# Wider modulation blocks and an earlier return of solved blocks in a two-layer hybrid attention and delta-rule trunk

## Chip, core and metric

One core of one Trainium2 chip runs the whole program. The metric is the device time in microseconds; the median of three runs of the kernel before is 2593.26.

## Reference

Two layers over 512 tokens (256 context, 256 latent) of width 2048, all in float32. Each layer computes a modulation (shift, scale and gate, 3 x 2048 columns each for latent and context) from two conditioning vectors, one input projection, two groups of eight heads (differential attention with rotary positions; a gated delta rule in both directions with a short convolution), and one output projection:

```
mod_lat = silu(c) @ w_ada + b_ada;  mod_ctx = silu(c_ctx) @ w_ada + b_ada
p  = (rmsnorm(x, norm_w) * (1 + sc) + sh) @ w_in
y_a = diff_post(diff_attend(q_l, k_all, v_all, lam), subln_w, lam_init, za)
m = tril_strict((k_beta @ k.T) * decay) + eye      # 64-token chunks
sol = triangular_solve(m, [v * beta, k_beta * exp(g)])
x  = x + gt * (concat([y_a, y_b]) @ w_out)
```

The context is updated in layer 0 only; layer 1 computes outputs for the latent tokens alone. The result is the RMS-normed latent stream.

## The kernel before

Engines are programmed one by one, and semaphores order them. A head of the input projection has eight tiles of 128 columns (AV, BQ, BK, AQ, AK, ZA, BV, ZB), each of two units of 8 x 128 rows: 16 units, 64 slots of four to a unit. In each slot TensorE does two row blocks of three matmuls (L1699 to L1701: w_hi by h_hi, w_hi by h_lo, w_lo by h_hi), and then what a hand-written plan puts into that slot for the head before ("fill"): transposes, Gram matrices (L1769, L1771), the merge of the inverse (L1780, L1789, L1790), the state recurrence, scores (L1858), the turn of the attention weights (L1865) and their product (L1872). ScalarE, VectorE, GpSimd and SyncE run the same slots with lists of their own, each in strict order of its list. A layer is nine bodies: projection of head 0 without fill, seven with both, and the last with the output projection in place of the input one.

Weights: SyncE loads a unit into one of two raw buffers (L526, `w_raw`) as soon as the unit two before it has been split; ScalarE rounds it to w_hi (L607, `split_hi`), VectorE subtracts for w_lo (L1060, `split_lo`), both three units ahead of TensorE (`LEAD`).

The inverse of the delta rule starts from 16 x 16 blocks. SyncE takes them to partitions through DRAM (L540, L543, `blocks_to_partitions`, in front of the load of unit 7), VectorE solves them in slots 12 to 15 of layer 0 (L293 to L309), SyncE brings them back (L548, L553, `blocks_back`, in front of the load of unit 10), and VectorE transposes them (L1312) in slots 20 and 21. TensorE's first merge step (L1780) is at slot 22.

Modulation columns that are not needed at the start (layer 0's gate, layer 1's all) are made in 64 blocks of 128 columns, six a head in layer 0 (slots 9, 14, 18, 46, 51, 57) and two a head in layer 1 (10, 17). For each block ScalarE loads 2048 x 128 weights in two DMAs (L912), TensorE multiplies with 16 matmuls of 32 columns on four column strips (L1639), ScalarE copies the result (L626) and issues the next load, TensorE turns it (L1648), and VectorE adds the bias. The first three blocks of a head in layer 0 use PSUM banks G0 and G1, the others A0 and A1.

In the last body the output projection's tiles n go to PSUM bank PJ + n % 2 (L1959 to L1961). ScalarE loads x (`part_load`, L933), VectorE adds gate x product (L1517), ScalarE stores (`part_store`, L944). The two head rows that come last are multiplied after it, in 16 products (L1998 to L2000), each followed by VectorE's add (L1517), ScalarE's square (L1033) and GpSimd's running sum (L1602), which the next RMS norm needs (L1661). A table of decay factors is made at the start of each layer in slots 2 to 8 of its first body (`table_step`, L1724, L1732, L1737). In layer 1 the first two units are multiplied before that body, so its first eight slots hold no projection.

Of the kernel before, what the change touches and what calls it, by code (L numbers as in the profile page):

```python
# [150 lines left out]
def build_trunk(nc, x, c, ctx_in, c_ctx, w_ada, b_ada, norm_w, w_in, conv_w, dn_a_log, dn_dt_bias,  # L151
# [15 lines left out]
    with ExitStack() as ctx:  # L167
# [28 lines left out]

        arena_size = 20764
        arena = sb("arena", [P, arena_size])
# [112 lines left out]
        def ada_banks(early):  # L311
            return (bank(G0, P), bank(G1, 2)) if early else (bank(A0, P), bank(A1, 2))

# [126 lines left out]
        def last_unit(n):  # L440

            return n + 2 if n < 2 else 2 * n + 1

        def piece_slot(p):
# [154 lines left out]
        def _(act):  # L599
# [23 lines left out]
            def ada_copy(value, early):  # L623
                act.wait_ge(ada_used, value * 2)
                need(act, ada_turned, value - 1)
                nc.scalar.copy(ada_sb[:], ada_banks(early)[0]).then_inc(ada_copied, 1)  # L626
                act.wait_ge(ada_copied, value)
# [48 lines left out]
            for layer in range(DEPTH):  # L676
# [56 lines left out]
                def body(i, project, fill):  # L733
# [170 lines left out]
                    def ada(k):  # L904
                        ada_copy(i * ADA_IN[layer] + (ada_before(layer) + k + 1), k < ADA_EARLY[layer])
                        if k + 1 < ADA_IN[layer]:
                            ada_load(k + 1)

                    def ada_load(k):
                        lay, firstb = ada_block(layer, k)  # L910
                        for hf in range(2):
                            act.dma_start(ada_raw[:, hf], w_ada[lay].rearrange("(k p) n -> p k n", p=P)[  # L912
                                :, hf * HALF:(hf + 1) * HALF, bass.ds((i * 2 + (firstb + k % 2)) * P, P)]).then_inc(
                                    ada_loaded[RAW + hf], 16)
# [63 lines left out]
                    if project:  # L978
                        for t in (AV, BQ, BK, AK, BV):
                            put(8 * t + 8, evacuate, t)  # L980
                        put(8 * AQ + 8, evacuate, AQ)
                        put(22, tanh, 0)
                        put(30, tanh, 1)
                        put(62, tanh, 2)
                        put(8 * ZA + 8, evacuate_z, 0, ZA)
                        put(0, ada_load, 0)
                        for k, s in enumerate(ADA_SLOT[layer]):
                            put(s + 1, ada, k)
                        if isinstance(i, int) and i == 0:
                            put(3, table_step, 0)  # L990
                            put(6, table_step, 1)
                            put(8, table_step, 2)
                            put(12, load_g, 0, 0)
                    if not project:
                        put(63, y_hi_last, 1)
                        for n in range(KT):
                            put(out_slot(n), part_store, n)
                            if n + 4 < KT:
                                put(min(out_slot(n) + 2, SLOTS - 1), part_load, n + 4)
                        for u in range(OUT_UNITS):  # L1000
                            put(piece_slot(2 * u), split_hi, 0, first + u + LEAD, OUT_HEADS if u + LEAD < OUT_UNITS else HALF)
                    for s in range(SLOTS):
                        if project and s % 4 == 1:
                            split_hi(i, base + 2 + s // 4 + LEAD)
                        for f, a in plan.get(s, ()):
                            f(*a)
# [48 lines left out]
        def _(vec):  # L1055
# [28 lines left out]
            def mod_column(value, lay, blk, early):  # L1084

                vec.wait_ge(ada_turned, value)
                tt(mod[:, lay, bass.ds(blk, 1), :].rearrange("p o v -> p (o v)"), ada_banks(early)[1],
                   vecs[:, 1, bass.ds(blk + lay * 3 * KT, 1)].to_broadcast([P, 2]), ALU.add).then_inc(mod_ready, 1)
                vec.wait_ge(mod_ready, value)
# [67 lines left out]
            for layer in range(DEPTH):  # L1157
# [49 lines left out]
                def body(i, project, fill):  # L1207
# [215 lines left out]
                    def ada(k):  # L1423
                        lay, firstb = ada_block(layer, k)
                        mod_column(i * ADA_IN[layer] + (ada_before(layer) + k + 1), lay, i * 2 + (firstb + k % 2),
                                   k < ADA_EARLY[layer])
# [56 lines left out]
                    if project:  # L1483
# [7 lines left out]
                        for k, s in enumerate(ADA_SLOT[layer]):  # L1491
                            put(s + 3, ada, k)
                        if isinstance(i, int) and i == 0:
                            put(2, table_step, 0)
                            put(4, table_step, 1)
                            put(6, table_step, 2)
                            put(8, table_step, 3)
                    if not project:
# [14 lines left out]
                def add_product(n, dst):  # L1513

                    for v in range(c0 // 2, 2):
                        seg = slice(v * N_CTX, (v + 1) * N_CTX)
                        m = V.scalar_tensor_tensor(dst[:, seg], ps[:, PJ + n % 2, seg], mod[:, layer, 2 * KT + n, v:v + 1],  # L1517
                                                   dst[:, seg], ALU.mult, ALU.add)
# [92 lines left out]
        def _(pe):  # L1611
# [18 lines left out]

            def ada_multiply(slots, loads, prior, out_):

                need(pe, ada_copied, prior)
                for half in range(2):
                    pe.wait_ge(slots[half][1], loads[half])
                    for k in range(HALF):
                        kt = half * HALF + k
                        j = kt % 4
                        last = mm(out_[32 * j:32 * j + 32], c_T[:, kt, :], slots[half][0][:, k, :],  # L1639
                                  start=kt < 4, stop=kt >= KT - 4)  # L1640
                        if k == HALF - 1:
                            last.then_inc(ada_used, 1)

            def ada_turn(value, out_):

                pe.wait_ge(ada_copied, value)
                need(pe, mod_ready, value - 1)
                mm(out_, ada_sb[:], sel, start=True, stop=True).then_inc(ada_turned, 1)  # L1648

# [37 lines left out]
            for layer in range(DEPTH):  # L1687
# [52 lines left out]
                def body(i, project, fill):  # L1740
# [150 lines left out]
                    def ada(k):  # L1891
# [6 lines left out]
                        loads = [i * (16 * ADA_IN[layer]) + 16 * (at_start[hf] + n + 1) for hf in range(2)]  # L1898
                        sl = [(ada_raw[:, hf], ada_loaded[RAW + hf]) for hf in range(2)]
                        v = i * ADA_IN[layer] + (first_loads + k)  # L1900
                        ada_multiply(sl, loads, v, ada_banks(k < ADA_EARLY[layer])[0])

# [31 lines left out]
                    if project:  # L1934
                        for n, s in enumerate(ROTATE[layer]):
                            put(s, rotate, n)
                        for k, s in enumerate(ADA_SLOT[layer]):
                            put(s, ada, k)
                            put(s + 2, ada_t, k)
                        if isinstance(i, int) and i == 0:  # L1940
                            put(2, table_step, 0)
                            put(5, table_step, 1)
                            put(8, table_step, 2)
                    def out_piece(p):
# [3 lines left out]
                        if p % 2 == 0:  # L1948
                            pe.wait_ge(w_split, u + 1)
                        if p == 0:  # L1950
                            pe.wait_ge(evacuated, (layer + 1) * LAYER_TILES)
                        if p % 2 == 0 and half == 0 and n >= 2:
                            pe.wait_ge(out_added, layer * 2 * KT + n - 1)
                        for k in (range(0, 4), range(4, OUT_HEADS))[p % 2]:
                            kt = half * HALF + k
                            if n == 0:
                                pe.wait_ge(y_split, layer * Y_STEPS + y_group_of[kt] + 1)
                            o = ps[:, PJ + n % 2, c0 * P:]
                            mm(o, w_hi[:, u % SPLIT, k], h_hi[:, kt, c0 * P:], start=kt == 0, stop=False)  # L1959
# [29 lines left out]
                for n in range(KT):  # L1989
# [4 lines left out]
                    for m, k in enumerate((OUT_HEADS, OUT_HEADS + HEADS)):  # L1994
                        hi, lo = [w[:, u % SPLIT].rearrange("p k n -> p (k n)")[:, (4 * m + col) * P:(4 * m + col + 1) * P]
                                  for w in (w_hi, w_lo)]
                        o = ps[:, PJ + n % 2, c0 * P:]
                        mm(o, hi, h_hi[:, k, c0 * P:], start=m == 0, stop=False)  # L1998
# [42 lines left out]
```

## Time and profile before

| | |
|---|---|
| median of the runs | 2593.26 us (2592.95 to 2595.0) |
| the profiled execution | 2584.58 us |
| its span | 2582.8 us |
| mean granted clock of TensorE | 0.963 |
| TensorE matmul busy | 2337.6 us, 91% |
| a filled head of layer 0, from one L1780 wait to the next (594.68 to 742.11) | 147 us |
| VectorE, ScalarE, GpSimd busy | 54%, 36%, 5% |
| DMA, mean | 128 GB/s |

The span runs from the first to the last instruction of the profiled execution. Times in rows are microseconds from its start, and durations in microseconds unless they are called ns. Busy shares are means over stages that differ.

### The profile page before, as it was taken

How to read it: one execution, taken by the hardware profiler on the slowest of the kernel's cores; microseconds unless marked ns; L12 is line 12 of the kernel's file. 1: busy time of each engine (PE TensorE's matmuls, PEld its weight loads, DVE VectorE, ACT ScalarE, POOL GpSimd, SP SyncE). 2: the span in 40 equal slices, each digit the busy share in tenths (PEclk: the TensorE clock that was granted, in tenths of full speed). 3: DMA queues.
4: the chain of work that ended last, by engine and by line, in shares of the span. 5: the costliest groups of instructions: out<-in, count | busy, mean ns of one | idle time of the engine just before them, and what ended most of it. 6: DMA issues, size and time to landing. Idle time of an engine off the chain costs nothing. (4 is left out here: it accounts for less than half of the span.)

```text
span 2582.8 us, 40809 instructions
## 1 busy us (share of the span) xinstructions
PE 2337.6 (91%) x14870; PEld 1931.1 (75%) x14870; DVE 1394.7 (54%) x2377; ACT 927.3 (36%) x1727; POOL 136.8 (5%) x187
## 2 busy tenths in 40 slices
PE   6799898998989898998999878999999999999687
PEld 3278786877768686877778757788887878878686
DVE  1343655555454555555564354656566665766554
ACT  3433324242423324242422253433424244242423
POOL 0000000000001000000100020000000000000002
PEclk8899999999999999999999989999999999999898
DMA  8964434352434445252545415533434344343453
GB/s 321 353 188 130 111 107 126 89 134 78 123 100 124 110 110 131 73 149 73 168 121 160 147 57 156 127 102 96 128 83 120 91 108 113 96 122 92 129 154 105
DMA packets 553603, 329.72 MB, mean 128 GB/s; under 512 B 48658, under 2 KB 517814, under 8 KB 552710
## 3 DMA queue, kind: packets, MB, share of 16 engines
q1 hardware_dynamic: 393174, 218.59, 30.5%
q10 hardware_dynamic: 160240, 109.13, 14.4%
q8 instruction: 94, 1.54, 0.2%
q14 instruction: 31, 0.25, 0.0%
q0 software_dynamic: 64, 0.20, 0.0%
HBM read 304.73 MB, written 23.13 MB: 127 GB/s over the span
## 5 line engine op out<-in xcount | busy, mean ns | idle before, releaser
L1699 PE MATMUL ps<-h_hi,w_hi 128*128 128x512 f32 (+1 forms) x2080 | 825.9, 397 | 17.6 <-DVE w_lo L1060 7.6
L1700 PE MATMUL ps<-h_lo,w_hi 128*128 128x512 f32 (+1 forms) x2080 | 765.1, 368 | 0.0
L1701 PE MATMUL ps<-h_hi,w_lo 128*128 128x512 f32 (+1 forms) x2080 | 764.2, 367 | 0.0
L1060 DVE TENSOR_TENSOR w_lo<-w_raw,w_hi 128x1024 fp32r<-128x1024 f32 (+1 forms) x332 | 399.2, 1202 | 345.9 <-ACT w_hi L607 280.0
L607 ACT CAST w_hi<-w_raw 128x1024 fp32r<-128x1024 f32 (+1 forms) x332 | 341.8, 1030 | 441.0 <-PE ps L1701 142.4
L1699 PEld LDWEIGHTS ps<-h_hi,w_hi 128*128 128x128 f32 x2080 | 398.4, 192 | 110.0 <-issue 42.6
L1701 PEld LDWEIGHTS ps<-h_hi,w_lo 128*128 128x128 f32 x2080 | 396.3, 191 | 67.5
L1700 PEld LDWEIGHTS ps<-h_lo,w_hi 128*128 128x128 f32 x2080 | 398.8, 192 | 46.5
L1060 DVE TENSOR_TENSOR arena<-arena,ps 128x512 f32<-128x512 f32 (+1 forms) x192 | 117.6, 640 | 107.4 <-PE ps L1790 106.0
L1959 PE MATMUL ps<-h_hi,w_hi 128*128 128x512 f32 (+1 forms) x448 | 160.6, 359 | 15.5 <-ACT arena L773 10.6
L1780 PE MATMUL ps<-arena 128*128 128x128 f32 x768 | 110.4, 290 | 55.6 <-DVE arena L1312 55.6
L1961 PE MATMUL ps<-h_hi,w_lo 128*128 128x512 f32 (+1 forms) x448 | 154.5, 345 | 0.0
L1960 PE MATMUL ps<-h_lo,w_hi 128*128 128x512 f32 (+1 forms) x448 | 154.4, 345 | 0.0
L1780 PEld LDWEIGHTS ps<-arena 128*128 128x128 f32 x768 | 104.7, 203 | 65.3 <-DVE arena L1312 60.6
L1559 POOL TENSOR_SCALAR small<-small 128x4 f32<-128x4 f32 (+3 forms) x51 | 20.5, 402 | 2358.9 <-DVE small L1413 1060.2
L1228 DVE SCALAR_TENSOR_TENSOR arena<-arena,convh 128x512 f32<-128x512 f32 (+1 forms) x192 | 135.7, 707 | 7.0 <-DVE arena L309 1.0
L1790 PE MATMUL ps<-arena 128*128 128x128 f32 x768 | 132.7, 275 | 0.0
L848 ACT ACTIVATE arena<-ps,hcol 128x128 f32<-128x128 f32 x128 | 40.1, 364 | 208.5 <-PE ps L1808 208.5
L1790 PEld LDWEIGHTS ps<-arena 128*128 128x128 f32 x768 | 111.1, 192 | 2.5
L1959 PEld LDWEIGHTS ps<-h_hi,w_hi 128*128 128x128 f32 x448 | 88.6, 198 | 27.7 <-issue 14.7
L1789 PE MATMUL ps<-arena 128*128 128x128 f32 x512 | 99.6, 276 | 6.5 <-DVE arena L1060 6.5
L1961 PEld LDWEIGHTS ps<-h_hi,w_lo 128*128 128x128 f32 x448 | 88.5, 198 | 9.2
(191 smaller groups left out, 2740.4 us busy)
## 6 DMA issues: line engine op xcount, KB each, us to landing
w_raw<-in_w_in SPq DMA_DIRECT2D x260, 512.0 KB, 4.1
ada_raw<-in_w_ada ACTq DMA_DIRECT2D x128, 512.0 KB, 5.1
w_raw<-in_w_out SPq DMA_DIRECT2D x64, 448.0 KB, 3.7
arena<-in_w_ada SPq DMA_DIRECT2D x27, 512.0 KB, 8.3
w_raw<-in_w_ada SPq DMA_DIRECT2D x19, 512.0 KB, 8.5
ada_raw<-in_w_ada SPq DMA_DIRECT2D x18, 512.0 KB, 8.3
arena<-decay_rows ACTq DMA_DIRECT2D x16, 512.0 KB, 5.7
x_channel_major<-arena ACTq DMA_DIRECT2D x1, 4096.0 KB, 17.5
```

The source lines that it names most:

```text
L607: nc.scalar.copy(w_hi[:, u % SPLIT, 0:tiles], w_raw[:, s, 0:tiles]).then_inc(w_hi_ready, 1)
L1060: return V.tensor_tensor(o, a, b, op)
L1228: m = V.scalar_tensor_tensor(acc, src, w, acc, ALU.mult, ALU.add)
L1699: mm(o, w_hi[:, s, k], h_hi[:, kt, t0:], start=kt == 0, stop=False)
L1700: before_last = mm(o, w_hi[:, s, k], h_lo[:, kt, t0:], start=False, stop=False)
L1701: last = mm(o, w_lo[:, s, k], h_hi[:, kt, t0:], start=False, stop=kt == KT - 1)
L1780: last = mm(quads(GX[d])[:, cc], m_T[:, d, cc], inv[:, d, cc], start=True, stop=True)
L1789: mm(quads(GX[d])[:, cc], inv_T[:, d, cc], prod[:, d, cc], start=True, stop=True)
L1790: last = mm(quads(GT[d])[:, cc], prod[:, d, cc], inv_T[:, d, cc], start=True, stop=True)
L1959: mm(o, w_hi[:, u % SPLIT, k], h_hi[:, kt, c0 * P:], start=kt == 0, stop=False)
L1960: mm(o, w_hi[:, u % SPLIT, k], h_lo[:, kt, c0 * P:], start=False, stop=False)
L1961: last = mm(o, w_lo[:, u % SPLIT, k], h_hi[:, kt, c0 * P:], start=False, stop=kt == HALF + OUT_HEADS - 1)
```

## The change

- Modulation: 32 pairs of blocks in place of 64 blocks. Each slot now holds one half of the contraction for 256 columns (8 matmuls, two DMAs with rows twice as long); copy, turn (two matmuls) and add come once a pair. Slots in layer 0 are 9, 12, 16, 19, 46, 52 with the first four in the early banks, in layer 1 10 and 16.
- `blocks_back` stands in front of the load of unit 9 in layer 0, not of unit 10.
- Output projection: tile n uses bank PJ + (n + 1) % 2; tile 0 waits for all but the last of the projection's tiles to be copied, tile 1 for the last. ScalarE's list has its splits in front of stores; stores come one slot after the add and loads three slots later than before.
- Layer ends: VectorE's split stands behind the add of n = 2, 6, 10, 14, not in front of the add of n = 0, 4, 8, 12.
- The table of layer 1 is made in slots 9 to 15.

```diff
-        ada_sb = sb("ada_sb", [P, P])
+        ada_sb = sb("ada_sb", [P, 2 * P])
...
-        arena_size = 20764
+        arena_size = 20488
...
-        ADA_SLOT, ADA_EARLY = {0: (9, 14, 18, 46, 51, 57), 1: (10, 17)}, {0: 3, 1: 2}
-        BLOCKS_OUT, BLOCKS_BACK = {0: 7, 1: 7}, {0: 10, 1: 10}
+        TABLE = {0: 0, 1: 7}
+        ADA_SLOT, ADA_EARLY = {0: (9, 12, 16, 19, 46, 52), 1: (10, 16)}, {0: 4, 1: 2}
+        BLOCKS_OUT, BLOCKS_BACK = {0: 7, 1: 7}, {0: 9, 1: 10}
...
+        def out_bank(n):
+            return PJ + (n + 1) % 2
...
                     def ada(k):
-                        ada_copy(i * ADA_IN[layer] + (ada_before(layer) + k + 1), k < ADA_EARLY[layer])
+                        value = i * ADA_IN[layer] + (ada_before(layer) + k + 1)
+                        act.wait_ge(ada_used, value * 2)
+                        if k % 2:
+                            ada_copy(value, k < ADA_EARLY[layer])
                         if k + 1 < ADA_IN[layer]:
                             ada_load(k + 1)
...
-                        for n in range(KT):
-                            put(out_slot(n), part_store, n)
-                            if n + 4 < KT:
-                                put(min(out_slot(n) + 2, SLOTS - 1), part_load, n + 4)
                         for u in range(OUT_UNITS):
                             put(piece_slot(2 * u), split_hi, ...)
+                        for n in range(KT):
+                            put(min(out_slot(n) + 1, SLOTS - 1), part_store, n)
+                        for n in range(KT - 4):
+                            put(min(out_slot(n) + 5, SLOTS - 1), part_load, n + 4)
...
                 for n in range(KT):
                     if n % 4 == 0:
-                        if n == 0 or layer < DEPTH - 1:
-                            split_lo(0, first + OUT_UNITS + n // 4 + LEAD)
                         vec.wait_ge(old_loaded[n // 4], 16 * (layer + 1))
                     vec.wait_ge(last_product, layer * KT + n + 1)
                     add_product(n, xT[:, n])
                     vec.wait_ge(out_added, (2 * layer + 1) * KT + n + 1)
+                    if n % 4 == 2 and (n == 2 or layer < DEPTH - 1):
+                        split_lo(0, first + OUT_UNITS + n // 4 + LEAD)
...
-            def ada_multiply(slots, loads, prior, out_):
+            def ada_multiply(half, loads, prior, out_):
                 need(pe, ada_copied, prior)
-                for half in range(2):
-                    pe.wait_ge(slots[half][1], loads[half])
-                    for k in range(HALF):
-                        kt = half * HALF + k
+                for hf in range(2):
+                    pe.wait_ge(ada_loaded[RAW + hf], loads[hf])
+                    for j in range(HALF // 2):
+                        kt = half * HALF + hf * HALF // 2 + j
...
-                        if p == 0:
+                        if p % 2 == 0 and half == 0 and n == 0:
+                            pe.wait_ge(evacuated, (layer + 1) * LAYER_TILES - 1)
+                        if p % 2 == 0 and half == 0 and n == 1:
                             pe.wait_ge(evacuated, (layer + 1) * LAYER_TILES)
```

## Rows read from the trace of the kernel before

**Rows 1.** The page, busy time, share and instructions of each engine.
```profile
PE 2337.6 (91%) x14870; PEld 1931.1 (75%) x14870; DVE 1394.7 (54%) x2377; ACT 927.3 (36%) x1727; POOL 136.8 (5%) x187
```
**Rows 2.** Waits of TensorE, whole span: total us, times, longest.
```profile
PE ps L1959 <- ACT arena L773: 10.6, 2, 5.5
PE ps L1639 <- DMA ada_raw<-in_w_ada: 7.9, 9, 1.7
...
PE ps L1732 <- DVE arena L1190: 7.5, 2, 7.0
```
**Rows 3.** Waits of TensorE, 290 to 1195, the filled heads of layer 0.
```profile
PE ps L1780 <- DVE arena L1312: 52.0, 7, 7.9
PE ps L1865 <- DVE arena L1407: 8.4, 6, 2.9
```
**Rows 4.** Timeline, 576 to 600: start, duration, instruction, [idle before it].
```profile
578.43 0.19 DVE L309 TENSOR_SCALAR arena<-arena 64x64 f32<-64x64 f32 x1
...
580.51 1.02 ACTq L912 DMA_DIRECT2D ada_raw<-in_w_ada  x2
...
581.82 0.37 SPq L526 DMA_DIRECT2D w_raw<-in_w_in  x1
582.24 0.90 SPq L548 DMA_DIRECT2D s_blocks<-arena  x1
...
588.91 3.64 SPq L553 DMA_DIRECT2D arena<-s_blocks  x8
593.91 0.71 DVE L1312 STREAM_TRANSPOSE arena<-arena 128x512 f32<-128x512 f32 x1 [9.86 <-DMA arena<-s_blocks]
...
594.68 2.07 PE L1780 MATMUL ps<-arena 128*128 128x128 f32 x8 [7.92 <-DVE arena L1312]
```
**Rows 5.** DMA issues: count, KB each, median us to landing.
```profile
w_raw<-in_w_in SPq DMA_DIRECT2D x260, 512.0 KB, 4.1
ada_raw<-in_w_ada ACTq DMA_DIRECT2D x128, 512.0 KB, 5.1
...
s_blocks<-arena SPq DMA_DIRECT2D x16, 64.0 KB, 1.9
```
**Rows 6.** Timeline, 556 to 575: a modulation load and who waits.
```profile
561.65 1.02 ACTq L912 DMA_DIRECT2D ada_raw<-in_w_ada  x2
...
562.28 0.48 SPq L543 DMA_DIRECT2D arena<-m_blocks  x1
...
567.43 0.64 PE L1639 MATMUL ps<-ada_raw,c_T 128*32 128x128 f32 x16
568.62 0.17 DVE L293 TENSOR_TENSOR arena<-arena 64x14 f32<-64x14 f32 x1 [4.18 <-DMA arena<-m_blocks]
...
568.91 0.65 PE L1639 MATMUL ps<-ada_raw,c_T 128*32 128x128 f32 x16 [0.83 <-DMA ada_raw<-in_w_ada]
```
**Rows 7.** Windows: busy PE, PEld, DVE, ACT, POOL; granted clock; DMA share, GB/s.
```profile
594.00:599.00 5.00, 4.32 (x17) 3.85 (x18) 4.33 (x8) 0.63 (x1) 0.00 (x0) 0.57 0.00 0
```
**Rows 8.** Timeline of TensorE, 653 to 656: a turn.
```profile
654.36 0.37 PE L1648 MATMUL ps<-cst,ada_sb 128*128 128x2 f32 x2
654.59 0.48 PE L1699 MATMUL ps<-h_hi,w_hi 128*128 128x512 f32 x1
```
**Rows 9.** Timeline, 1466 to 1512, the end of layer 0.
```profile
1473.68 0.79 PE L1998 MATMUL ps<-h_hi,w_hi 128*128 128x512 f32 x1 [4.81 <-DVE arena L1517]
...
1482.50 1.23 DVE L1060 TENSOR_TENSOR w_lo<-w_raw,w_hi 128x1024 fp32r<-128x1024 f32 x1 [2.37 <-ACT w_hi L607]
...
1510.73 1.44 PE L1661 MATMUL ps<-cst,arena 128*128 128x1 f32 x6 [3.47 <-POOL arena L1602]
```
**Rows 10.** Groups by line and form, GpSimd: busy us, mean ns, idle before.
```profile
L1602 POOL TENSOR_TENSOR arena<-arena 128x512 f32<-128x512 f32 x16 | 20.5, 1281 | 41.3 <-ACT arena L1033 40.7 <-POOL arena L1602 0.2
```
**Rows 11.** Timeline, 2436 to 2448, output part of layer 1.
```profile
2439.79 1.09 DVE L1060 TENSOR_TENSOR w_lo<-w_raw,w_hi 128x896 fp32r<-128x896 f32 x1 [2.09 <-ACT w_hi L607]
...
2447.03 1.12 PE L1865 MATMUL ps<-cst,arena 128*128 128x128 f32 x4 [7.51 <-DVE arena L1407]
```

More of the change, by code:

```diff
@@ L1491, in body @@
                         for k, s in enumerate(ADA_SLOT[layer]):
-                            put(s + 3, ada, k)
+                            if k % 2:
+                                put(s + 3, ada, k)
                         if isinstance(i, int) and i == 0:
[L1494 to L1497, printed above, removed]
+                            put(TABLE[layer] + 2, table_step, 0)
+                            put(TABLE[layer] + 4, table_step, 1)
+                            put(TABLE[layer] + 6, table_step, 2)
+                            put(TABLE[layer] + 8, table_step, 3)
                     if not project:
@@ L1629, in turn_x @@
                     last.then_inc(x_turned, 1)
-            def ada_multiply(slots, loads, prior, out_):
+            def ada_multiply(half, loads, prior, out_):
                 need(pe, ada_copied, prior)
-                for half in range(2):
-                    pe.wait_ge(slots[half][1], loads[half])
-                    for k in range(HALF):
-                        kt = half * HALF + k
-                        j = kt % 4
-                        last = mm(out_[32 * j:32 * j + 32], c_T[:, kt, :], slots[half][0][:, k, :],
+                for hf in range(2):
+                    pe.wait_ge(ada_loaded[RAW + hf], loads[hf])
+                    for j in range(HALF // 2):
+                        kt = half * HALF + hf * HALF // 2 + j
+                        last = mm(out_[32 * j:32 * j + 32], c_T[:, kt, :], ada_wide_rows(hf)[:, j],
                                   start=kt < 4, stop=kt >= KT - 4)
-                        if k == HALF - 1:
-                            last.then_inc(ada_used, 1)
+                    last.then_inc(ada_used, 1)
             def ada_turn(value, out_):
                 pe.wait_ge(ada_copied, value)
-                need(pe, mod_ready, value - 1)
-                mm(out_, ada_sb[:], sel, start=True, stop=True).then_inc(ada_turned, 1)
+                need(pe, mod_ready, value - 2)
+                for b in range(2):
+                    last = mm(out_[:, 2 * b:2 * b + 2], ada_sb[:, b * P:(b + 1) * P], sel, start=True, stop=True)
+                last.then_inc(ada_turned, 2)
             pe.wait_ge(staged, 2)
@@ L1898, in ada @@
                         loads = [i * (16 * ADA_IN[layer]) + 16 * (at_start[hf] + n + 1) for hf in range(2)]
-                        sl = [(ada_raw[:, hf], ada_loaded[RAW + hf]) for hf in range(2)]
-                        v = i * ADA_IN[layer] + (first_loads + k)
-                        ada_multiply(sl, loads, v, ada_banks(k < ADA_EARLY[layer])[0])
+                        v = i * ADA_IN[layer] + (first_loads + k // 2 * 2)
+                        ada_multiply(k % 2, loads, v, ada_banks(k < ADA_EARLY[layer])[0])
                     def ada_t(k):
@@ L1938, in body @@
                             put(s, ada, k)
[L1939 removed]
+                            if k % 2:
+                                put(s + 2, ada_t, k)
                         if isinstance(i, int) and i == 0:
[L1941 to L1943 removed]
+                            put(TABLE[layer] + 2, table_step, 0)
+                            put(TABLE[layer] + 5, table_step, 1)
+                            put(TABLE[layer] + 8, table_step, 2)
                     def out_piece(p):
```

34 lines of the change are left out of this document (18 added, 16 removed).

## Prediction

> **What bounds the kernel now.** I read the page first: the reader is to see that TensorE is busy 91% of the span, with VectorE at 54% and ScalarE at 36% [rows 1]. No other engine is near its limit, so the time is TensorE's work plus the stretches in which it stands still, and an edit counts only if it shortens one of these. The second view is therefore the waits of TensorE over the whole span [rows 2] and over the heads of layer 0 [rows 3]. Of its idle time after start-up, the largest single item is 52.0 us: seven waits, one in each filled head of layer 0, for the transpose of the solved blocks (L1312). Each is 7 to 8 us in a head of 147 us. All the others named in [rows 2, 3] are 4 to 15 us in total. The third view is the timeline of one such head, to see what the wait hangs on; the fourth the granted clock behind it; the rest are the same for each other edit.
>
> **1. Blocks back one unit sooner.** In [rows 4] VectorE ends the substitution at 578.6. SyncE's queue has the load of unit 9 in front of the solved blocks (unit count of the head), and that load waits for a split until 581.82; the store of the blocks goes out at 582.24, is waited for until 588.91, the eight reads take 3.64 to issue, and the transpose runs at 593.91, 1.36 after the last issue. TensorE then goes on at 594.68, after 7.92 idle. With the blocks in front of load 9 the store goes out at about 578.7. A store with nothing in its way lands in 1.9 [rows 5], so: 578.7 + 1.9 + 3.7 + 1.4 = 585.7, plus 0.7 for the transpose = 586.4. TensorE reached the place at 594.68 - 7.92 = 586.76. So the wait could go wholly. It is not free of company: in the store's way at 582.24 were the weight load of 581.82 and a modulation load of ScalarE's queue at 580.51, and it took 6.7 instead of 1.9. In the new order the load of the fourth modulation piece is issued by ScalarE at about 577 to 578 (slot 17), just ahead of the store. I leave 5 of the 52 (0.7 a head) and take **-47**; bounds: -52 (all gone), and -25 if the store still takes 6.7 at 578.7, which would leave about half. What is moved back is weight load 9: it now stands behind the store, its wait and eight reads, so it goes out near 585 instead of 581.8. It is split at slot 25, three slots (2.3 us each, 147 by 64) after the place at which TensorE waited, so at about 593.5; with 4.1 to land [rows 5] there are some 4 to 5 us to spare, and I cost it at nothing. GpSimd's queue is not touched.
> On what lies in a transfer's way the Trainium skill says otherwise than these rows ("DMA: Bandwidth & Descriptors", section "Queues, rings and completion order"): each DMA engine takes turns between the queues that have work, packet by packet, so ScalarE's loads would slow the small store but not hold it. By that the five left over go as well and the blocks come in sooner too; this is rival B. The rows do not bear it out well: the read of the blocks issued at 562.28, behind two ScalarE loads at 561.65, was used only at 568.62 [rows 6].
>
> **2. The clock behind those waits.** Between 594 and 599 the granted clock is 0.57 [rows 7]: TensorE had been idle for 7.9, and then ran near its 1.2 GHz level for most of them; the mean of the span is 0.963. With 4.32 busy in these 5 us, 4.32 x 0.43 = 1.86 is lost; I take 1.75, seven times: **-12** (bounds 0 and -14). It comes only if the wait becomes short; how long an idle time leaves the clock alone these rows do not show, so the near bound is 0.
>
> **3. Modulation pieces of 256 columns.** The 64 blocks become 32 pairs; each pair is two calls (half of the contraction each), one copy, one turn of two matmuls, one add. A call had 32 instructions on 128 columns and now has 16 on 256: the same columns, 0.65 for each half call [rows 6]. Turns: one turn takes 0.23 until the next matmul starts [rows 8]; a pair took 0.46, now one start and twice the instructions, about 0.35: 32 x 0.11 = 3.5. I take **-4** with a little for fewer instructions (bounds 0 and -8). Copies and adds lie on engines with room.
> The DMAs carry the same bytes. But slots change in layer 0 from 9, 14, 18, 46, 51, 57 to 9, 12, 16, 19, 46, 52. A load is issued by ScalarE one slot after a piece and must be in at the next: it had 4 slots from 9 to 14 and now has 2 from 9 to 12, and 2 from 16 to 19. In [rows 6] the load issued at 561.65 is what TensorE waits for at 568.91 (idle 0.83), 7.3 later; that piece was at slot 14 and began at 567.43; two slots of 6 x 0.23 and a turn sooner, slot 12 comes at 567.43 - 2.8 - 0.3 = 564.3. The median of these loads is 5.1, that of a weight load 4.1 [rows 5]; I take 4.7 for the landing, between the two, as it now ends before the weight load behind it begins. Issued 0.4 sooner, as no copy is in front, it is in at 566.0, and the second half (wanted at 564.8) waits 1.2. The waits for this load were 7.9 in all [rows 2]; I put 1.2 at slot 12 and 0.2 to 0.5 at slot 19 in seven heads, and 3 to 4 in the unfilled first one: about 15, so **+7** (bounds -5, if longer rows land sooner, and +25, if it lands 7.3 after issue as in [rows 6]). In layer 1 the second piece moves from slot 17 to 16 with over 2 us in hand: nothing. The add of the first block left the substitution's way and the blocks arrive sooner, so the wait for VectorE's mix at L1865 (8.4 [rows 3]) should halve, and with it some clock: **-5** (bounds 0 and -8).
>
> **4. Layer ends.** In layer 0's last 16 products VectorE splits w_lo ahead of every fourth add. At 1482.50 it starts this 2.37 late, waiting for ScalarE's half, which itself comes only after the last square; the add comes behind it, and TensorE waits for the add. The first wait of this kind is 4.81, at 1473.68 [rows 9]. The split now comes two adds later, when w_hi has long been there. What is late next: GpSimd's running sum, 16 x 1.28 [rows 10] = 21 with its gaps, and TensorE's 6 x 0.23 = 1.4 a product. The sum ended for TensorE at 1510.73. Started at 1472 and paced at 1.4 to 1.5, it ends at 1495 to 1496: -15. Layer 1 has only the first of these splits and half the tokens; of the 4.81 I take -3 for it. Together **-18** (bounds -10 and -21).
>
> **5. Output part.** Tile 0 now goes to the other PSUM bank and no longer waits for z_b's copy: 10.6 in two waits [rows 2]. What ends last then is the split of y (h_lo), made by the same two engines just before the copy; no row parts the two, so the bounds are 0 and -10.6, and as the code hands both out in slots 0 and 1 I take a small part: **-3**. ScalarE's split no longer queues behind a store that waits for the add. In layer 0's output part TensorE has no wait for it: nothing. In layer 1's it idles 7.51 [rows 11] for VectorE's mix, and 7 us before its end VectorE had itself stood 2.09 for such a split; two or three of them go by half, with the smaller waits around: **-5** (0 to -9). The stores go out one slot later and the loads three later; a part loaded 5 slots after tile n is used some 15 slots after it, so this is covered.
>
> **6. Table of layer 1** moves 7 slots. There the first 8 slots have no projection, so TensorE idled 7.05 for L1190 (7.5 with layer 0's [rows 2]). It can now start unit 2 when VectorE has split it, about 2.4 after the last unit; slots 9 to 15 have 256 columns only and give back 1 to 2: **-4** (0 to -7).
>
> **Sum:** -47 - 12 - 4 + 7 - 5 - 18 - 3 - 5 - 4 = -91. The profiled execution took 2584.6 (span 2582.8 and 1.8 around it), so 2493.6 in its terms. The median of the runs is 8.7 above it, 2593.3: forecast **2502**. All best bounds together give -52 - 14 - 8 - 5 - 8 - 21 - 10.6 - 9 - 7 = -135, 2459; the terms do not err together, and half of that distance either way, 2480 to 2524, is the likely one's own range.
>
> **Rivals.**
> A, forecast. 0.55.
> B, the two queues share and nothing holds the blocks: L1780 and L1865 waits go wholly, -5 and -3.4 more: about 2493. For it: no row shows a small transfer in front of a load being slow. Against: [rows 6]. 0.16.
> C, the blocks are still late: store behind the fourth piece's load, the reads beside the fifth's. Each head keeps 3 to 4 us idle and the clock dip: -25 and 0 in place of -47 and -12: 2502 + 34 = about 2536. For it: 6.7 for a 64 KB store in [rows 4]. 0.14.
> D, the modulation loads become the wait of layer 0: 4.9, their whole landing, exposed at slots 12 and 19, less what the blocks' wait hid: 7 x (9.8 - 1.7) = +57 on my +7 term, minus 7 x 0.7: about 2554. For it: only two slots each. Against: slots there carry fillers and last over 2 us. 0.08.
> E, within 0.2%: the idle time is only handed from one wait to the next in each head. 0.03.
> F, slower: SyncE stands in front of weight load 9 until the blocks are solved. If the substitution ended more than 5 us later than now, load 9 would starve the split, and as two raw buffers chain the loads, every unit behind it. To eat 91 in seven heads it must end 18 us later (5 to spare and 91 / 7 = 13 of loss); nothing in [rows 4, 6] is that late. At 20 it gives about 2607. 0.04.
> Measurement can tell about 0.2% (5 us) from no change. Faster 0.93, same 0.03, slower 0.04. The range 2478 to 2540 takes in A, B and C, about 85%.
>
> **What would show it.** Right: L1780's wait for L1312 in layer 0 under 1 us a head; granted clock 1.00 where it was 0.57; the store of s_blocks some 3 us before the weight load; L1639's wait for its DMA grown to about 15; the last GpSimd sum of layer 0 within 25 us of the first; L1732 near nothing. Wrong: the store landing more than 5 us after issue (C); L1639 waits above 4 us (D); a wait of L1699 for w_lo near slot 36 (F); or a new wait in slots 22 to 33, where VectorE and TensorE hand the merge back and forth in every slot and which the old wait gave VectorE time for.

## The result, and the profile after

The changed kernel took 2517.3 us (median; 2515.01 to 2523.75), the kernel before 2593.1 beside it: ratio 0.9716, interval 0.9697 to 0.9735, 76 us or 2.8% faster. The forecast was 2502 with 2478 to 2540. The direction and the range held, and the gain is some 15 short of the 91 of the sum. The profiled execution took 2515.0 against 2584.6, 69.6 less. That the range held is in part luck: terms of the sum that came out too large and others that came out too small offset each other; which ones is what the experiments ask.

The page, busy time of each engine (answers to [rows 1]):
```profile
PE 2322.5 (92%) x13846; PEld 1893.7 (75%) x13846; DVE 1392.0 (55%) x2345; ACT 922.2 (37%) x1695; POOL 147.3 (6%) x187
```
TensorE has 15 us less of work, the instructions saved by wider blocks and some time at the full clock; the rest of the gain is idle time. Waits of TensorE over the whole span (answers to [rows 2, 3]; L1651 is the old L1639, L1793 the old L1780, L1878 the old L1865, L1974 the old L1959, L1745 the old L1732, L1712 the old L1699):
```profile
PE ps L1878 <- DVE arena L1419: 29.3, 16, 7.1
PE ps L1793 <- DVE arena L1324: 17.4, 9, 3.5
...
PE ps L1974 <- DVE h_lo L1072: 13.1, 6, 4.2
PE ps L1651 <- DMA ada_raw<-in_w_ada: 12.8, 17, 1.5
...
PE ps L1674 <- POOL arena L1615: 8.9, 2, 6.3
...
PE ps L1745 <- DVE arena L1202: 5.4, 1, 5.4
PE ps L1660 <- ACT ada_sb L634: 5.3, 7, 1.0
```
and in the window 290 to 1147, the filled heads of layer 0:
```profile
PE ps L1793 <- DVE arena L1324: 15.0, 7, 3.5
PE ps L1651 <- DMA ada_raw<-in_w_ada: 9.2, 12, 1.2
PE ps L1802 <- DVE mod L1072: 3.2, 3, 1.2
```
The 52.0 us of the blocks became 15.0, not 5. The L1865 waits of these heads (8.4 in [rows 3]) are gone. L1651 waits grew by 5, as forecast. Two waits are new: L1802 for the pair's add on VectorE, and L1660 for ScalarE's copy of the pair in layer 1.

One head of layer 0 in the timeline shows why 15 are left (answers to [rows 4]; L557 and L562 are the blocks' store and reads, L535 the weight load, L924 the modulation load):
```profile
561.87 0.94 ACTq L924 DMA_DIRECT2D ada_raw<-in_w_ada  x2
562.45 0.19 DVE L309 TENSOR_SCALAR arena<-arena 64x64 f32<-64x64 f32 x1
562.72 0.47 SPq L557 DMA_DIRECT2D s_blocks<-arena  x1
...
566.96 3.65 SPq L562 DMA_DIRECT2D arena<-s_blocks  x8
...
569.93 0.94 ACTq L924 DMA_DIRECT2D ada_raw<-in_w_ada  x2
...
570.93 8.06 SPq L535 DMA_DIRECT2D w_raw<-in_w_in  x2
...
573.91 0.71 DVE L1324 STREAM_TRANSPOSE arena<-arena 128x512 f32<-128x512 f32 x1 [5.83 <-DMA arena<-s_blocks]
...
574.67 1.16 PE L1793 MATMUL ps<-arena 128*128 128x128 f32 x8 [1.75 <-DVE arena L1324]
```
The store now goes out 0.1 behind the solve, as forecast. But a modulation load of 1 MB (two DMAs of 512 KB, the weights of one modulation slot or "piece") was issued 0.9 ahead of it, and the store is done 4.2 after its issue, not 1.9; the next modulation load goes out among the last reads, and the transpose comes 3.3 behind the last issue, not 1.4. From the solved blocks to the transpose it is 11.3 us where the forecast had 7.1 and the kernel before 15.3.

The granted clock behind three of these waits (answers to [rows 7], with its columns; the clock is the third number from the end):
```profile
436.10:441.10 5.00, 5.00 (x23) 4.56 (x24) 4.54 (x8) 0.63 (x1) 0.00 (x0) 0.66 0.36 101
574.70:579.70 5.00, 4.77 (x28) 3.93 (x28) 4.54 (x8) 0.63 (x1) 0.00 (x0) 1.00 0.34 94
713.50:718.50 5.00, 4.80 (x28) 3.93 (x28) 4.54 (x8) 0.63 (x1) 0.00 (x0) 1.00 0.39 111
```
Idle times of 1.85, 1.75 and 1.79 precede them. The first was followed by most of 5 us at the 1.2 GHz level, the other two were not. In four of the seven heads the clock was at 0.66 to 0.69, in three at 1.00.

### The profile page after: what moved, and what is told of

The parts are those of the page before. It is cut to its first block and busy times, and to the rows that moved or that the text cites. A ratio compares the mean times of both kernels' runs of the same rounds, so it can differ in the third digit from the quotient of the medians.

```text
span 2513.2 us, 38542 instructions
## 1 busy us (share of the span) xinstructions
PE 2322.5 (92%) x13846; PEld 1893.7 (75%) x13846; DVE 1392.0 (55%) x2345; ACT 922.2 (37%) x1695; POOL 147.3 (6%) x187
## 5 line engine op out<-in xcount | busy, mean ns | idle before, releaser
L1712 PE MATMUL ps<-h_hi,w_hi 128*128 128x512 f32 (+1 forms) x2080 | 824.3, 396 | 19.1 <-DVE w_lo L1072 10.9
L1712 PEld LDWEIGHTS ps<-h_hi,w_hi 128*128 128x128 f32 x2080 | 399.1, 192 | 123.0 <-issue 52.4
L1713 PEld LDWEIGHTS ps<-h_lo,w_hi 128*128 128x128 f32 x2080 | 399.9, 192 | 47.7
L1974 PE MATMUL ps<-h_hi,w_hi 128*128 128x512 f32 (+1 forms) x448 | 160.0, 357 | 13.4 <-DVE h_lo L1072 13.1
L1803 PE MATMUL ps<-arena 128*128 128x128 f32 x768 | 132.6, 275 | 0.0
L1793 PE MATMUL ps<-arena 128*128 128x128 f32 x768 | 105.2, 281 | 17.4 <-DVE arena L1324 17.4
L1793 PEld LDWEIGHTS ps<-arena 128*128 128x128 f32 x768 | 100.6, 196 | 25.5 <-DVE arena L1324 20.8
L1802 PE MATMUL ps<-arena 128*128 128x128 f32 x512 | 99.7, 276 | 10.6 <-DVE arena L1072 7.4
L1974 PEld LDWEIGHTS ps<-h_hi,w_hi 128*128 128x128 f32 x448 | 87.8, 196 | 26.7 <-issue 12.5
```

What stands on the lines that cost most here:

```text
L1712: mm(o, w_hi[:, s, k], h_hi[:, kt, t0:], start=kt == 0, stop=False)
L1713: before_last = mm(o, w_hi[:, s, k], h_lo[:, kt, t0:], start=False, stop=False)
L1793: last = mm(quads(GX[d])[:, cc], m_T[:, d, cc], inv[:, d, cc], start=True, stop=True)
L1802: mm(quads(GX[d])[:, cc], inv_T[:, d, cc], prod[:, d, cc], start=True, stop=True)
L1803: last = mm(quads(GT[d])[:, cc], prod[:, d, cc], inv_T[:, d, cc], start=True, stop=True)
```

## The experiments

Twelve runs. The kernel before was measured in each group: 2589.1, 2588.8 and 2591.4. Times across groups are compared by ratio. The changed kernel, run again unedited in the second group, had 0.9704; with the first 0.9716 I take 0.971, and a ratio higher by 0.001 is 2.6 us. By the intervals, a difference from the changed kernel is known to about 0.002, 5 us, either way.

| run | median us | ratio | interval |
|---|---|---|---|
| blocks_alone | 2546.9 | 0.9834 | 0.9816 to 0.9851 |
| table_unmoved | 2521.5 | 0.9736 | 0.9721 to 0.9751 |
| piece_17 | 2512.3 | 0.9707 | 0.9685 to 0.9728 |
| pieces_15_18 | 2525.8 | 0.9750 | 0.9735 to 0.9766 |
| after_again | 2512.3 | 0.9704 | 0.9689 to 0.9718 |
| small_loads | 2472.2 | 0.9540 | 0.9521 to 0.9559 |
| table_15 | 2512.4 | 0.9713 | 0.9692 to 0.9735 |
| pieces_15_19 | 2501.2 | 0.9657 | 0.9642 to 0.9672 |
| ends_unmoved | 2537.4 | 0.9788 | 0.9775 to 0.9802 |
| out_undone | 2525.1 | 0.9750 | 0.9735 to 0.9765 |
| mended | 2503.5 | 0.9659 | 0.9646 to 0.9672 |
| blocks_undone | 2536.9 | 0.9791 | 0.9776 to 0.9806 |

**The blocks, done alone and undone.** Two runs.
```diff
 # blocks_alone: the kernel before
-BLOCKS_OUT, BLOCKS_BACK = {0: 7, 1: 7}, {0: 10, 1: 10}
+BLOCKS_OUT, BLOCKS_BACK = {0: 7, 1: 7}, {0: 9, 1: 10}
 # blocks_undone: the changed kernel
-BLOCKS_OUT, BLOCKS_BACK = {0: 7, 1: 7}, {0: 9, 1: 10}
+BLOCKS_OUT, BLOCKS_BACK = {0: 7, 1: 7}, {0: 10, 1: 10}
```


> The kernel before with one edit: solved blocks come back in front of load 9 in layer 0. Theory (what is left of the wait in the changed kernel comes from ScalarE's modulation loads, which now go out 0.9 us ahead of the store and just ahead of the last read): with the old slots the load nearest to the store is issued 1.8 us behind it, so the store lands in about 2 us, L1780 waits under 1.2 us in each head of layer 0, and the granted clock behind it is near 1.00: about 2539 (-54). Rival (the solved blocks need 12 us from the last step of the solve to TensorE whatever stands beside them): L1780 waits 1.8 to 3.5 in each head, the clock still falls in half of them: about 2549 (-44).

> The changed kernel with the blocks back in front of load 10, as before. Theory (the edit is worth 42 us alone, and the other edits of layer 0 do not depend on it): L1793 waits 6 to 8 a head, about 2554 (+42). Rival (with the new slots the modulation load goes out before load 9 and the blocks, so the late blocks cost more): over 2560. Rival of the other side (TensorE comes to the place later by the pieces' waits, which hide part): under 2545.

Alone the edit gave 42 to 43 us, so the rival's number held. Its reason held only in part: the old slots leave the store free (first read 2.0 behind the solve), but the modulation load that follows it at 1.8 goes out just ahead of the reads. In this run's timeline the transpose comes 9.8 behind the end of the solve at 566.73:
```profile
566.54 0.19 DVE L309 TENSOR_SCALAR arena<-arena 64x64 f32<-64x64 f32 x1
566.81 0.47 SPq L548 DMA_DIRECT2D s_blocks<-arena  x1
...
568.62 1.05 ACTq L912 DMA_DIRECT2D ada_raw<-in_w_ada  x2
568.75 4.76 SPq L553 DMA_DIRECT2D arena<-s_blocks  x8
...
576.53 0.71 DVE L1312 STREAM_TRANSPOSE arena<-arena 128x512 f32<-128x512 f32 x1 [4.37 <-DMA arena<-s_blocks]
...
577.30 1.16 PE L1780 MATMUL ps<-arena 128*128 128x128 f32 x8 [2.42 <-DVE arena L1312]
```
Taken back out of the changed kernel it cost only 21 (0.9791 less 0.971), half as much, and the rival of the other side had the right number. The waits of TensorE in blocks_undone, 290 to 1180:
```profile
PE ps L1793 <- DVE arena L1324: 32.2, 7, 5.1
PE ps L1651 <- DMA ada_raw<-in_w_ada: 10.4, 13, 2.4
```
So the new slots of the pieces had already taken the blocks' wait from 52.0 to 32.2, with the blocks where they were. Two things show in its timeline. TensorE comes to the place some 10 to 11 behind the solve instead of 8. And the modulation load that had stood 1.7 ahead of the late store [rows 4] now goes out 3.3 ahead of it (4.4 to 5.5 in five other heads), and the store and its wait take 4.2 (3.8 to 4.0 there) instead of 6.7. What it still waits behind is the weight load of its own queue, issued 0.4 ahead of it. Times from issue to landing (us, last number) of the three transfers, first in the kernel before (issued 580.4 to 583), then in blocks_undone (573.3 to 577.5):
```profile
ada_raw<-in_w_ada ACTq DMA_DIRECT2D x2, 512.0 KB, 6.1
w_raw<-in_w_in SPq DMA_DIRECT2D x1, 512.0 KB, 6.9
s_blocks<-arena SPq DMA_DIRECT2D x1, 64.0 KB, 6.7
```
```profile
ada_raw<-in_w_ada ACTq DMA_DIRECT2D x2, 512.0 KB, 4.2
w_raw<-in_w_in SPq DMA_DIRECT2D x1, 512.0 KB, 4.4
s_blocks<-arena SPq DMA_DIRECT2D x1, 64.0 KB, 4.1
```
In both the store lands 0.1 to 0.2 behind that weight load (588.9 against 588.7, 580.9 against 580.8), and well behind the modulation load. The two edits take from the same wait, and the sum counted it once for each.

**Where the modulation loads stand.** Three runs on the changed kernel:
```diff
 # pieces_15_18, and pieces_15_19
-ADA_SLOT = {0: (9, 12, 16, 19, 46, 52), 1: (10, 16)}
+ADA_SLOT = {0: (9, 12, 15, 18, 46, 52), 1: (10, 16)}
+ADA_SLOT = {0: (9, 12, 15, 19, 46, 52), 1: (10, 16)}
 # small_loads, in ada_load
+few = 1 if layer == 0 else HALF // 2
-act.dma_start(ada_wide_rows(hf), w_ada...[:, first_k:first_k + HALF // 2, ...])
+act.dma_start(ada_wide_rows(hf)[:, :few], w_ada...[:, first_k:first_k + few, ...])
```


> The changed kernel with the third and fourth modulation pieces of layer 0 at slots 15 and 18, not 16 and 19. Theory (the store of the blocks is held by the load that is issued 0.9 us ahead of it): that load now goes out some 3 us ahead, the store lands in about 2 us, L1793 waits 0 to 0.5 in place of 1.8 a head and the clock no longer falls behind it: about 2502 (-15). Rival: the load of the fifth piece then stands in front of the eight reads, the idle time stays: within 3 of 2517.

> The changed kernel, but every modulation load in the heads of layer 0 brings only one of its four row blocks, a quarter of the bytes; TensorE multiplies what lies in the buffer, so the modulation is not that of the reference. Theory (the modulation loads hold the blocks' store and reads, and are themselves what L1651 waits for): L1651 waits under 2 in place of 12.8, L1793 under 2 in place of 17.4, and the clock does not fall behind it: about 2487 (-30). Rival (the blocks' way through DRAM is slow by itself, and the loads only make the pieces wait): L1793 keeps 15 and more, about 2506 (-11).

> The changed kernel with the third modulation piece of layer 0 at slot 15, not 16; its load then goes out some 3 us ahead of the blocks' store, not 0.9, and the fourth piece keeps slot 19. Theory (a load of 1 MB takes 4 to 5 us, and what stands behind it waits for the rest): the first read comes some 3 us after the solve in place of 4.4, L1793 waits under 0.5 a head, L1651 grows by 0.4 to 0.8 a head at slot 15: about 2507 (-10). Rival (idle time is only handed to L1651, as with slots 15 and 18, where its waits grew by 27): 2517 or more.

With slots 15 and 18 the blocks' wait for VectorE went away as expected and the kernel still became 10 us slower. The waits of TensorE from 290 to 1170 in pieces_15_18, and from 290 to 1147 in pieces_15_19:
```profile
PE ps L1651 <- DMA ada_raw<-in_w_ada: 32.9, 33, 2.7
```
```profile
PE ps L1651 <- DMA ada_raw<-in_w_ada: 19.0, 25, 2.2
```
Neither has a row for L1793 left. In the first, both the third and the fourth piece have two slots from issue to use, and the idle time of the blocks is handed to the pieces with more on top: the prediction's rival D, at a smaller size. In the second, three slots lie before slot 19: L1651 grows from 9.2 to 19.0, but L1793 loses its 15.0, and the time fell by 14 (0.9657; 11 in medians of the same group). The expectation had the right number with a wrong picture of the order: the load goes out 0.8 behind the store, not 3 ahead of it:
```profile
566.16 0.18 DVE L309 TENSOR_SCALAR arena<-arena 64x64 f32<-64x64 f32 x1
566.43 0.47 SPq L557 DMA_DIRECT2D s_blocks<-arena  x1
...
567.23 0.95 ACTq L924 DMA_DIRECT2D ada_raw<-in_w_ada  x2
568.36 3.65 SPq L562 DMA_DIRECT2D arena<-s_blocks  x8
...
573.89 0.71 DVE L1324 STREAM_TRANSPOSE arena<-arena 128x512 f32<-128x512 f32 x1 [0.84 <-DMA arena<-s_blocks]
...
577.80 1.05 PE L1793 MATMUL ps<-arena 128*128 128x128 f32 x8
```
Here the chain is what the forecast had: read 2.0 behind the end of the solve (566.34), transpose 7.6, against a forecast of 7.1, and TensorE does not wait. The granted clock is 1.00 in the five us behind L1793 in all seven heads. With a quarter of the bytes (small_loads, which leaves out three quarters of these weights, so that its result is not the reference's) no wait at all is left in this stretch, neither for the blocks nor for the pieces. One head, from 411.7:
```profile
411.70:544.50 132.80, 132.80 (x792) 107.58 (x791) 78.72 (x132) 48.16 (x96) 6.55 (x9) 1.00 0.31 86
```
TensorE is busy for all 132.8 us, at full clock, where a head of the changed kernel takes 138.0 to 139.4. The transpose comes 7.2 to 7.7 behind the solve, in place of 11.3. The 44 us of small_loads below the changed kernel (40 in medians of the group, where its expectation had 30) are the whole price of these loads, waits, clock and unfilled head together. That settles the cause: the way of the blocks through DRAM is not slow by itself.

**Layer 1's second piece, and the table.** Three runs on the changed kernel:
```diff
 # piece_17
-ADA_SLOT = {..., 1: (10, 16)}
+ADA_SLOT = {..., 1: (10, 17)}
 # table_unmoved, and table_15
-TABLE = {0: 0, 1: 7}
+TABLE = {0: 0, 1: 0}
+TABLE = {0: 0, 1: 15}
```


> The changed kernel with the second modulation piece of a head of layer 1 at slot 17, as before, not 16. Theory: ScalarE's copy of the pair stands in slot 17 behind the exponentials of the second scores and TensorE's turn in slot 18 waits for it 0.9 us a head; one slot later nothing is in front of it: L1660 waits near 0 and 5 to 8 us less, about 2511. Rival: the loss of layer 1 (8.3 us over its heads) comes from elsewhere, a copy of 256 columns and a turn of two matmuls; then 2517.

> The changed kernel with the table of layer 1 in slots 2 to 8, as before. The prediction's step: the move gave 4 us, so this is 4 slower, 2521. Rival, from the two traces set side by side at the same projection matmul (65.8 us ahead in front of the table, 64.4 behind it): the move gave nothing or cost 1.4, as the chain through ScalarE's two loads of a function table is as long as three short slots in either place: 2516 to 2517.

> The changed kernel with the table of layer 1 in slots 17 to 23, not 9 to 15; these slots have 512 columns. Theory (the chain of the table through VectorE and ScalarE takes some 9 us and is covered only by slots that long): L1745 waits under 1 in place of 5.4, 5 to 8 us less, about 2510. Rival (ScalarE's and VectorE's part of the chain delays the splits and copies of the head instead): within 2 of the changed kernel.

piece_17 took the wait L1660 away, and its median did not move (0.9707 against 0.971); in its trace six heads of layer 1 take 654.4 together, in the changed kernel's second execution 655.8, a difference too small for the medians. The loss of layer 1 that it was to mend was partly no property of the kernel: set side by side at the same projection matmul, the first execution of the changed kernel lost 8.3 us on the kernel before over the heads of layer 1, the second only 2.7. The difference comes in steps of 1.5, one head each. The same 110.9 us of both (changed kernel, then again):
```profile
1856.50:1967.40 110.90, 104.25 (x678) 89.07 (x677) 69.64 (x121) 41.73 (x81) 6.92 (x9) 0.98 0.37 104
```
```profile
1856.50:1967.40 110.90, 104.04 (x688) 89.89 (x687) 70.88 (x123) 41.73 (x81) 6.93 (x9) 1.00 0.38 104
```
Beside the first head, where every trace has 0.98, the clock fell in three heads of the first and in none of the second. What stays is 0.4 us a head, some 3 in all, which the forecast had at nothing.

table_unmoved was 7 slower (0.9736), 5 either way, so the sign of the forecast's step (4) held and its size is not contradicted, but its reason did not hold. TensorE waits 5.35 for the table's chain in the new place and 6.94 in the old one, but by slot 15 the old place is 1.8 us better by the traces side by side, as the shorter slots give all of it back. The loss of 6.9 comes behind that, in slots 16 to 18. ScalarE, in table_unmoved:
```profile
1513.12 1.04 ACT L616 CAST w_hi<-w_raw 128x1024 fp32r<-128x1024 f32 x1 [7.23 <-DMA w_raw<-in_w_in]
1514.07 0.37 ACT L634 COPY ada_sb<-ps 128x256 f32<-128x256 f32 x1
...
1514.49 1.01 PE L1660 MATMUL ps<-cst,ada_sb 128*128 128x2 f32 x4 [3.64 <-ACT ada_sb L634]
```
ScalarE's split of slot 17 waits 7.23 for its weights (why they come so late there was not followed up), the pair's copy stands behind it, and TensorE's turn waits for the copy. In the kernel before that second block was copied and turned one slot later, and there was no such wait. table_15 removed the table's idle time (L1745 from 5.4 to 0.3) and did not move the median (0.9713); its trace gives back 4.7 of 9.8 in the slots behind, and the rest is within what executions differ by.

**The layer ends and the output part, undone.**
```diff
 # ends_unmoved
 if n % 4 == 0:
+    if n == 0 or layer < DEPTH - 1:
+        split_lo(0, first + OUT_UNITS + n // 4 + LEAD)
...
-    if n % 4 == 2 and (n == 2 or layer < DEPTH - 1):
-        split_lo(0, first + OUT_UNITS + n // 4 + LEAD)
 # out_undone: out_bank(n) = PJ + n % 2, tile 0 waits for all tiles,
 # part_store at out_slot(n), part_load at + 2, both in front of split_hi
```


> The changed kernel with VectorE's splits of the layer ends in front of every fourth add again. The prediction's step: -18 (layer 0 -15, layer 1 -3), so 17 to 18 slower than the changed kernel beside it (2512), about 2530; the wait for GpSimd's sum (L1674) is shorter and the products wait for their adds. Rival: the sum of GpSimd is the bound either way, and it is under 8 slower.

> The changed kernel with the output part as before: bank PJ + n % 2, tile 0 waiting for all tiles of the projection, ScalarE's splits behind the stores, stores one slot and loads three slots sooner. The prediction's two steps: -3 and -5, so 8 slower than the changed kernel beside it, 2520. Rival, from the traces side by side (layer 0: 47.7 us ahead at its last projection, 52.3 at the end of its output part; layer 1: 56.1 and 64.7): 12 to 13 slower, 2525.

The layer ends are worth 20 (0.9788), the output part 10 (0.9750), both within the noise of the 18 and 8 of the forecast; 10 lies between the 8 and the rival's 12 to 13. With the splits back in front of the adds the old waits came back: 4.75, 2.16, 2.16 and 2.15, beside the 4.81 of [rows 9]. In out_undone's trace the stretch from the last projection matmul to the end of the output part takes 2.9 more in layer 0 than in the changed kernel's, 1.9 of it ahead of the first tile (the bank), and 9.6 more in layer 1 (6.3 more than in the changed kernel's second execution); other stretches of that execution were faster by a few us, as single executions are.

**All three edits.** Slots 15 and 19 in layer 0, slot 17 in layer 1, the table from slot 17:


> The changed kernel with three edits of the earlier runs: pieces of layer 0 at slots 9, 12, 15, 19, 46, 52; second piece of layer 1 at 17; table of layer 1 from slot 17. Theory (they lie in different stretches and add up): -11 as measured, -3 in the heads of layer 1 and -5 for the table by the traces, about 2494. Rival (the last two gave nothing that their medians showed): 2501, as with the first alone.

The rival was right: 0.9659, the same as with the first edit alone. The best version is the changed kernel with slots 9, 12, 15, 19, 46, 52: 2501.2, 3.4% faster than before.

**The changed kernel again:**


> The changed kernel itself, unedited, as the reference of this group and to see how much its heads of layer 0 differ from one execution to the next: 2514 to 2520; each head of layer 0 from 137.5 to 141 us, as the modulation load goes out just ahead of the blocks' store or just behind it.

Its time was 2512.3 (2511.1 to 2518.75), a little below the range; its heads of layer 0 took 138.3 to 140.5, inside theirs. Its last projection matmul of layer 0 ended 43.2 ahead of the kernel before's, the first execution's 49.1 (the 47.7 in the expectation of out_undone was read ahead of slot 57, where the kernel before still had a piece to do); so single traces differ by 6 there, and only medians decide on a few us.

## Why the forecast was right, and where it was off

**Step 1, the blocks: the term that failed.** "I leave 5 of the 52 (0.7 a head)" gave -47; the trace has 15.0 left, and the edit with its clock was worth 42 alone and 21 as the last one, against 59. The step saw the fourth piece's load go out just ahead of the store, and priced that at 0.7 a head, by no row. The 6.7 of [rows 4] was the price of two loads, ScalarE's 1.7 ahead and SyncE's own weight load 0.4 ahead; the step named both, and no row parted them. The modulation load alone made it 4.2 against 1.9 free, and the reads paid 1.9 more for the load of the fifth piece among them (not for weight load 9: in small_loads that goes out as close behind the reads, and the transpose still comes 1.3 to 1.4 behind their last issue). So the chain was 4.2 longer in the head shown, where the sum allowed 0.7. The step's own bound was also a little off: with 6.7 its numbers give a wait of 4.4 a head, a gain of 21 and not 25. Weight load 9 was rightly costed at nothing: no wait for weights appeared, and rival F didn't come. TensorE's own arrival at L1793 was forecast at 8.2 behind the solve and came at 10.3, which hid part of the error.

**Step 2, the clock.** The fall went where the wait really went (pieces_15_19: 1.00 in all seven heads) and about half of it went here: summed over the seven stretches of 5 us, what the clock lacks of 1.00 is 13.9 us before and 6.7 in the changed kernel, so about 7 of the 12 by this estimate. Behind the 6.4 to 8.0 us of before the clock was 0.50 to 0.70, behind 4.3 to 5.1 (blocks_undone) 0.50 to 0.67. Behind 1.3 to 3.5 (the changed kernel's two executions and blocks_alone, 20 heads) it was 1.00 in 11 and 0.66 to 0.69 in 9, and the length does not part them: 1.00 behind one wait of 3.53, 0.66 behind one of 1.81. One wait of 4.42 in the second execution had 0.50 behind it. The near bound of 0 was too careful, the far one too sure.

**Step 3, the pieces.** The forecast had -4 + 7 - 5 = -2. The L1651 waits came to 12.8 against 15, and the L1865 waits of layer 0's filled heads went wholly. What the step lacked is that its slots also move the load away from the late store and delay TensorE. After the blocks are mended, the pieces are worth about +5 (-75 in all, less 43 for the blocks alone and 37 for the other parts undone), which the intervals of three differences can't tell from nothing; before that, up to -17. The new waits at L1802 (3.2) and L1660 (5.3) are part of it. Layer 1, costed at nothing, has 3 of it.

**Steps 4 and 5** were sized well: 18 against 20, 8 against 10. What is late next was named rightly: GpSimd's sum. TensorE waits 6.32 for it behind the last product, where before it waited 3.47:
```profile
1419.85 12.45 POOL L1615 TENSOR_TENSOR arena<-arena 128x512 f32<-128x512 f32 x8 [23.25 <-ACT arena L1045]
1432.45 12.45 POOL L1615 TENSOR_TENSOR arena<-arena 128x512 f32<-128x512 f32 x8
...
1444.96 1.86 PE L1674 MATMUL ps<-cst,arena 128*128 128x1 f32 x8 [6.32 <-POOL arena L1615]
```
Sixteen adds end to end, 25.1 in place of the forecast's 23 to 24.

**Step 6, the table:** right sign, 4 against 7, by another mechanism than the one given. The wait of 5.4 stayed where the step had it near nothing.

In all, the parts of layer 0 and the pieces were forecast at -61 and gave -38; the ends, the output part and the table at -30 and gave -37. Of the signs that the prediction named for being right, three did not come: L1793 under 1 us a head (2.1), the clock at 1.00 (in three heads of seven) and the table's wait near nothing. Of the rivals, C had the right mechanism for the shortfall (the store behind the fourth piece's load, the reads beside the fifth's) and about twice its size: 2.1 idle a head (15.0 by 7), not 3 to 4. B didn't hold. The page "DMA: Bandwidth & Descriptors" of the Trainium skill, section "Queues, rings and completion order", has each DMA engine go from queue to queue packet by packet. By the landing times of the trace, the two DMAs of the modulation load in the timeline above (issued at 561.87 and 562.41) land 3.4 and 4.3 later, at 565.3 and 566.7, and the 64 KB store of 562.72 lands at 566.9: it ended no sooner than the load. In blocks_alone a smaller transfer did pass one, as that rule allows: the first 8 KB read (568.75) lands at 572.8, 0.9 ahead of the DMA issued 0.13 before it (568.62):
```profile
ada_raw<-in_w_ada ACTq DMA_DIRECT2D x1, 512.0 KB, 5.0
arena<-s_blocks SPq DMA_DIRECT2D x1, 8.0 KB, 4.0
```
It is slowed all the same, 4.0 against a median of 1.7 before. Why the store gains less than the read from such turns stays open; what helped was to issue the store first (pieces_15_19: 1.9, with the load 0.8 behind it).

## What to carry to other kernels

Price a small transfer on the critical path by what its own and another queue issue in the microseconds ahead of it, each by itself, with the loaded duration from the trace and not the free one; then move the load, not only the small transfer. Two edits that shorten the same wait must not be added up: undo each from the final kernel as well as doing it alone. An idle time cut into short pieces can cost less than one long wait: here the clock held behind 11 of 20 waits of 1.3 to 3.5 us, and behind none of the 14 of 4.2 and more in the kernel before and blocks_undone.

## What the runs showed of the hardware

GpSimd's add became slower as it was packed beside VectorE's splits. The group of the sum in layer 0's end, 1410 to 1450:
```profile
L1615 POOL TENSOR_TENSOR arena<-arena 128x512 f32<-128x512 f32 x16 | 23.7, 1480 | 24.6 <-ACT arena L1045 23.2
```
Before, the same 16 adds took 20.5, 1281 ns each [rows 10], and in ends_unmoved again 20.5. The 3.2 more lie in four adds of 1.96 to 2.09 that run into a w_lo split of 1.2 to 1.4. This agrees with the Trainium skill, "SBUF — State Buffer", section "SBUF: two separate sides": a VectorE operation with two inputs in SBUF, as this split, and a GpSimd one that reads SBUF take turns on one pair of ports, for a whole instruction each. Here it costs 3 us on the path, as this sum is what ends last.

The granted clock fell in one execution of a kernel and not in the next, in heads of layer 1 whose waits are none over 2.1 us, each fall worth 1.5 us (a head of 110.9 in place of 109.3). In layer 0, too, the length of a wait did not say whether the clock would fall (step 2).
